# GpSimd's low halves ahead of the gate products, and a reordered even mixer, in a two-block float32 network on one core

## The reference

```python
def even_mixer(x, ...):
    p = x @ w_in
    ...
    o = gla_chunked(q, k, v, log_a)
    o = o * lax.rsqrt(jnp.mean(jnp.square(o), -1, keepdims=True) + LN_EPS) * gla_norm_g
    gla_out = o.reshape(B, T, GLA_VW) * jax.nn.silu(gg)
    ...
    kk = heads(k * rwkv_k_k, RWKV_HEADS)
    kk = kk / jnp.maximum(jnp.sqrt(jnp.sum(jnp.square(kk), -1, keepdims=True)), 1e-12)
    k = k * (1.0 + (a - 1.0) * rwkv_k_a)
    y = rwkv7_scan(r_h, heads(decay, RWKV_HEADS), k_h, v_h, -kk, kk * a_h)
    mu = y.mean(-1, keepdims=True)
    var = jnp.square(y - mu).mean(-1, keepdims=True)
    y = (y - mu) * lax.rsqrt(var + RWKV_LNX_EPS) * rwkv_lnx_g + rwkv_lnx_b
    bonus = jnp.sum(r_h * k_h * rwkv_r_k, -1, keepdims=True) * v_h
    rwkv_out = (y + bonus).reshape(B, T, RWKV_W) * g
    return jnp.concatenate([gla_out, rwkv_out], -1) @ w_out
```

## Time and profile before

| | |
|---|---|
| time, median of 3 runs | 3585.91 us (3582.16 to 3587.43) |
| time of the profiled execution | 3586.25 us |
| its span, instructions | 3584.5 us, 49478 |
| PE busy | 3252.6 us (91%), mean granted clock 0.954 |
| VectorE busy | 2184.6 us (61%) |
| ScalarE busy | 1499.0 us (42%) |
| GpSimd busy | 535.2 us (15%) |
| DMA | 158 GB/s, mean over the span |

### The profile page before, as it was taken

One profiled execution on the slowest core, in us unless ns is written; L12 is line 12 of the kernel. 1 busy time (PEld: TensorE's weight loads), 2 busy tenths in 40 slices (PEclk: granted clock), 3 DMA queues, 4 the chain that ended last, 5 costly groups with the idle time before them and its releaser, 6 DMA issues.

```text
span 3584.5 us, 49478 instructions
## 1 busy us (share of the span) xinstructions
PE 3252.6 (91%) x20412; PEld 2873.0 (80%) x20412; DVE 2184.6 (61%) x3104; ACT 1499.0 (42%) x1677; POOL 535.2 (15%) x275
## 2 busy tenths in 40 slices
...
GB/s 183 138 185 162 212 152 182 151 105 163 181 169 195 157 185 158 132 2 118 165 155 116 113 236 192 187 188 188 153 35 143 176 129 137 153 228 179 188 188 127
DMA packets 87677, 565.23 MB, mean 158 GB/s; under 512 B 10176, under 2 KB 10192, under 8 KB 23584
## 3 DMA queue, kind: packets, MB, share of 16 engines
...
## 4 chain that ended last, share of the span: by engine, by line
PE 46%; DVE 6%; POOL 4%; ACT 4%; issue 1%; DVEq 0%; ACTq 0%
PE bank L1841 7%; PE bank L1843 7%; PE bank L1842 7%; PE bank L1820 6%; PE bank L1821 6%; PE bank L1822 6%; POOL w_lo L1488 3%; ACT w_hi L1935 2%; PE bank L1803 1%; PE bank L1543 1%; PE bank L1544 1%; PE bank L1545 1%; DVE hot_i L2517 1%; PE bank L1567 1%; PE bank L1568 1%
## 5 line engine op out<-in xcount | busy, mean ns | idle before, releaser
L1935 ACT ACTIVATE w_hi<-raw 128x2048 fp32r<-128x2048 f32 x290 | 555.4, 1916 | 838.5 <-PE bank L1843 395.6
L2199 DVE TENSOR_TENSOR w_lo<-raw,w_hi 128x2048 fp32r<-128x2048 f32 x222 | 531.6, 2396 | 609.2 <-ACT w_hi L1935 609.1
L875 DVE TENSOR_TENSOR w_lo<-raw,w_hi 128x2048 fp32r<-128x2048 f32 x202 | 462.4, 2292 | 413.1 <-ACT w_hi L687 409.7
L1820 PE MATMUL bank<-act_hi,w_hi 128*128 128x256 f32 x2048 | 598.8, 292 | 60.8 <-POOL w_lo L1488 55.2
L687 ACT ACTIVATE w_hi<-raw 128x2048 fp32r<-128x2048 f32 x202 | 386.5, 1915 | 545.8 <-PE bank L464 371.4
L1821 PE MATMUL bank<-act_lo,w_hi 128*128 128x256 f32 x2048 | 586.2, 286 | 0.0
L1822 PE MATMUL bank<-act_hi,w_lo 128*128 128x256 f32 x2048 | 585.8, 286 | 0.0
L1820 PEld LDWEIGHTS bank<-act_hi,w_hi 128*128 128x128 f32 x2048 | 399.0, 195 | 66.4 <-POOL w_lo L1488 60.2
L1841 PE MATMUL bank<-w_hi,c_hi 128*128 128x512 f32 x1024 | 405.0, 396 | 0.0
L1842 PE MATMUL bank<-w_lo,c_hi 128*128 128x512 f32 x1024 | 405.0, 395 | 0.0
L1843 PE MATMUL bank<-w_hi,c_lo 128*128 128x512 f32 x1024 | 405.0, 395 | 0.0
...
## 6 DMA issues: line engine op xcount, KB each, us to landing
...
```

What stands on the lines that cost most here:

```text
L875: nc.vector.tensor_tensor(w_lo[:, k % SPLIT, :], raw[:, k % RAW, :], w_hi[:, k % SPLIT, :].bitcast(F32), ALU.subtract).then_inc(lo_ready, 1)
L1820: mm(dst, wh[:, ws], act_hi[:, kk_, :], start=kk_ == 0 and jj == 0, stop=False)
L1935: A.activation(hi_of(k), raw[:, k % RAW, :], ACT.Copy).then_inc(hi_ready, 1)
L2199: V.tensor_tensor(lo_of(k), raw[:, k % RAW, :], hi_of(k).bitcast(F32), ALU.subtract).then_inc(lo_ready, 1)
```

## The change

GpSimd's part. In the gate stage the low half of tile p+1 moves ahead of all weighings of tile p. Two tiles of the even mixer, 12 and 13 (the first output weights), are made by GpSimd instead of VectorE, and GpSimd waits for the step "z" of both halves before the first of them. `lo` moves out of `peer_layer`.

The norms of kk. PE's product with a 128x128 matrix that gave each row's sum over its head in the feature layout becomes one with two columns, which gives 8 sums per token in the token layout. ScalarE's root, VectorE's maximum and reciprocal work on 128x8 instead of 128x512; VectorE spreads the result over 512 columns, and PE transposes it back into PSUM (the new step "norm"), where the product with kk reads it. These instructions stand ahead of the state updates.

The GLA output. PE's `o` waits for the states alone, no more for "tilde" of the first half. ScalarE copies it to `ymix` (step "copied") and takes the squares there. VectorE's scaling is cut into six pieces, one behind the first product of each level.

The end of the chain. `fade[2]` is made behind the chain's first copy. The statistics of the first half stand behind the second new state, its centring behind the third copy, its last two instructions behind the third state.

```diff
+MIX_LO_BY_POOL = (EVEN_OUT, EVEN_OUT + 1)
...
-    _by = any(_t - _first in LO_BY_POOL for _first in PEER_UV)
+    _by = _t in MIX_LO_BY_POOL or any(_t - _first in LO_BY_POOL for _first in PEER_UV)
...
@@ gpsimd
+        pool.wait_ge(rw_pe, TT * RW_PE["z"])
+        for k in MIX_LO_BY_POOL:
+            lo(base + k)
         pool.wait_ge(tr_lo, 8)
         ln_load(0)
...
             for p in range(FIRST_GATED, LAST_GATED + 1):
-                for n, g in enumerate(mid_groups(p) + end_groups(p)):
+                if p + 1 in LO_BY_POOL:
+                    lo(first + p + 1)
+                for g in mid_groups(p) + end_groups(p):
                     if g + HOT < GROUPS:
                         weigh(g + HOT)
-                    if n == 0 and p + 1 in LO_BY_POOL:
-                        lo(p + 1)
@@ tensor
             for f in range(FT):
-                last = mm(psum[4 + t][:, f * P:(f + 1) * P], cst("same_head"), sq[:, f, HALVES[t]], start=True, stop=True)
+                last = mm(psum[4 + t][:, 2 * f:2 * f + 2], sq[:, f, HALVES[t]], cst("half"), start=True, stop=True)
...
+        for t in range(TT):
+            by_dve("norm", t)
+            for f in range(FT):
+                last = nc.tensor.transpose(psum[4 + t][:, f * P:(f + 1) * P], norm[:, t, f * P:(f + 1) * P], ident)
+            last.then_inc(rw_pe, 1)
         pe.wait_ge(even_dve, EVEN_DVE["states"])
-        by_dve("tilde", 0)
...
                 if t and n == 2:
-                    pe.wait_ge(even_dve, EVEN_DVE["gla"])
+                    pe.wait_ge(even_act, EVEN_ACT["copied"])
@@ scalar
             by_pe("bonus", t)
-            do(A.activation(norm[:, t, :], psum[4 + t][:, :], ACT.Sqrt), rw_act)
+            do(A.activation(rnorm[:, t, :], psum[4 + t][:, 0:RH], ACT.Sqrt), rw_act)
         act.wait_ge(even_pe, EVEN_PE["o"])
         for t in range(TT):
+            do(A.activation(ymix[:, t, 0:EW], psum[6 + t][:, :], ACT.Copy), even_act if t else None)
+        for t in range(TT):
             for h in range(GH):
...
@@ vector
         def split_lo(k):
-            if k < total:
+            if k < total and not LO_COUNT[k - base][0]:
...
+        for t in range(TT):
+            by_act("norm", t)
+            if t == 0:
+                by_pe("bonus", TT - 1)
+                do.also(V.tensor_copy(bonus[:, :, :], psum[7][:, 0:TT * RH].rearrange("p (t h) -> p t h", t=TT)))
+            do(V.tensor_scalar(rnorm[:, t, :], rnorm[:, t, :], 1e-12, None, ALU.max))
+            do(V.reciprocal(rnorm[:, t, :], rnorm[:, t, :]))
+            do(V.tensor_copy(norm[:, t, :].rearrange("p (h n) -> p h n", h=RH), bcast(rnorm[:, t, :].unsqueeze(2), [P, RH, RN])), rw_dve)
...
-        def gla_out():
+        def gla_out(n):
+            t, part = n // 3, n % 3
+            if part == 0:
+                dve.wait_ge(even_act, EVEN_ACT["std"])
+                if t == 0:
+                    do(V.reciprocal(small[:, 8:16], small[:, 8:16]))
+            if part == 2:
                 do(V.tensor_tensor(ymix[:, t, 0:EW], ymix[:, t, 0:EW], gsil[:, t, :], ALU.mult), even_dve if t else None)
+                return
+            for h in (2 * part, 2 * part + 1):
...
-            n0 = norm[:, t, :]
-            do(V.tensor_scalar(n0, n0, 1e-12, None, ALU.max))
-            do(V.reciprocal(n0, n0))
-            do(V.tensor_tensor(kk[:, :, ts], kk[:, :, ts], n0.rearrange("p (f s) -> p f s", f=FT), ALU.mult))
+            by_pe("norm", t)
+            do(V.tensor_tensor(kk[:, :, ts], kk[:, :, ts], psum[4 + t][:, :].rearrange("p (f s) -> p f s", f=FT), ALU.mult))
...
-        gla_out()
         eye = cst("eye64")
+        dve.wait_ge(even_pe, EVEN_PE["o"])
...
+            gla_out(n)
...
+            if n == 0:
+                end = (CHUNKS - 1) * CHUNK_T - 1
+                do.also(V.tensor_tensor(fade[2], ...))
+            if n == 2:
+                centre(0)
             if n < CHUNKS - 1:
                 dve.wait_ge(chain_pe, 2 * n + 2)
                 do(V.tensor_tensor(s_all[:, n, :, :], ...), chain_dve)
+            if n == 1:
+                statistics(0)
+            if n == 2:
+                finish(0)
+        statistics(1)
+        centre(1)
+        finish(1)
```

More of the change, by code:

```diff
@@ L225 @@
 LEVEL_STEPS = [f"{s}{n}" for n in range(LEVELS) for s in "xd"]
-RW_PE = steps("bonus", "nat", "lr", "x0", *LEVEL_STEPS[2:], "z", "y")
+RW_PE = steps("bonus", "norm", "nat", "lr", "x0", *LEVEL_STEPS[2:], "z", "y")
 RW_ACT = steps("decays", "norm", "nat", "z", "std")
-RW_DVE = steps("cumsum", "bonus", "tilde", "lr", *LEVEL_STEPS, "stats")
+RW_DVE = steps("cumsum", "bonus", "norm", "tilde", "lr", *LEVEL_STEPS, "stats")
 ODD_PE = steps("it", "index0", "index1", "qt", "logits0", "pt0", "o0", "logits1", "pt1", "o1")
@@ L1252, in second_block @@
     gv = sb("gv", [P, TT, EW], F32, gla)
+    gap2 = sb("gap2", [P, (CHUNKS - 1) * FT * P - TT * EW], F32, gla)
     gsil = sb("gsil", [P, TT, EW], F32, gla)
@@ L1475, in ln_load, with lo @@
             pool.dma_start(ln_rows_at[n][:, 1, :], ln_rows[2 * n + 1].partition_broadcast(P)).then_inc(ln_loaded, 16)
+        def lo(k):
+            pool.wait_ge(hi_ready, k + 1)
+            nc.gpsimd.tensor_tensor(lo_of(k), raw[:, k % RAW, :], hi_of(k).bitcast(F32), ALU.subtract).then_inc(lo_pool, 1)
+        pool.wait_ge(rw_pe, TT * RW_PE["z"])
+        for k in MIX_LO_BY_POOL:
+            lo(base + k)
         pool.wait_ge(tr_lo, 8)
@@ L1483, in peer_layer @@
             first, g0 = base + PEER_UV[layer], GROUPS * layer
-            def lo(q):
-                k = first + q
-                pool.wait_ge(hi_ready, k + 1)
-                nc.gpsimd.tensor_tensor(lo_of(k), raw[:, k % RAW, :], hi_of(k).bitcast(F32), ALU.subtract).then_inc(lo_pool, 1)
             def weigh(g):
@@ L1496, in peer_layer @@
                 if q in LO_BY_POOL:
-                    lo(q)
+                    lo(first + q)
             for g in range(HOT):
@@ L2338, in _ @@
                        even_dve if c == CH * TT - 2 and g == GP - 1 else None)
-        def gla_out():
-            dve.wait_ge(even_act, EVEN_ACT["std"])
-            do(V.reciprocal(small[:, 8:16], small[:, 8:16]))
-            for t in range(TT):
-                for h in range(GH):
-                    hs = slice(h * GDV, (h + 1) * GDV)
-                    do(V.scalar_tensor_tensor(out=ymix[:, t, hs], in0=psum[6 + t][:, hs], scalar=small[:, 8 + t * GH + h:9 + t * GH + h],
-                                              in1=erow[:, EROW["gla_g"]], op0=ALU.mult, op1=ALU.mult))
-                do(V.tensor_tensor(ymix[:, t, 0:EW], ymix[:, t, 0:EW], gsil[:, t, :], ALU.mult), even_dve if t else None)
+        def gla_out(n):
[5 more added lines that the diff above has]
+            if part == 2:
+                do(V.tensor_tensor(ymix[:, t, 0:EW], ymix[:, t, 0:EW], gsil[:, t, :], ALU.mult), even_dve if t else None)
+                return
+            for h in (2 * part, 2 * part + 1):
+                hs = slice(h * GDV, (h + 1) * GDV)
+                do.also(V.scalar_tensor_tensor(out=ymix[:, t, hs], in0=ymix[:, t, hs], scalar=small[:, 8 + t * GH + h:9 + t * GH + h],
+                                               in1=erow[:, EROW["gla_g"]], op0=ALU.mult, op1=ALU.mult))
+            do.settle()
         for t in range(TT):
@@ L2415, in _, with statistics @@
         do.settle()
-        end = (CHUNKS - 1) * CHUNK_T - 1
-        do(V.tensor_tensor(fade[2], bcast(cst("same_head").unsqueeze(1), [P, FT, P]), bcast(pinc[:, :, end:end + 1], [P, FT, P]), ALU.mult))
-        for n in range(CHUNKS):
-            t, c = n // CH, n % CH
-            cs = slice(c * CHUNK_T, (c + 1) * CHUNK_T)
-            dve.wait_ge(chain_pe, 2 * n + 1)
-            do(V.tensor_copy(uu[cs, t, :], psum[4 * t + 1][cs, :]), chain_dve)
-            if n < CHUNKS - 1:
-                dve.wait_ge(chain_pe, 2 * n + 2)
-                do(V.tensor_tensor(s_all[:, n, :, :], psum[4 * t + 2 + c][:, :].rearrange("p (f s) -> p f s", f=FT), fade[n], ALU.mult), chain_dve)
-        for t in range(TT):
+        def statistics(t):
             by_pe("y", t)
```

25 lines of the change are left out of this document (16 added, 9 removed).

## The result

The changed kernel takes 3535.82 us (median of 4 runs, 3533.29 to 3541.45) against 3586.55 us of the kernel before on the same chip: ratio 0.9863, 95% interval 0.9846 to 0.988. Its profiled execution took 3533.58 us against 3586.25, 52.7 us less. The first row of its page, busy time and share of the span, says that PE works no less, but stands less and runs faster: 92% of a span of 3531.9 us, with a mean granted clock of 0.959.

The account below looks back on a forecast made before the run. PE, by far the busiest engine, was taken as the bound, losing time to waits and clock drops. Gate stage 30.2, clock 16.1 and mixer 6.6 sum to 52.9 us, from 3586.25 to 3533.4; range 3517 to 3553.

Parts of the forecast that it names:

- Gate stage: Expert stage: GpSimd's low half ahead of the weighings shortens ten PE stalls a layer, 30.2 us over two layers.
- The foreseen exception: Gate stage: VectorE's low half gets ahead of the first weighing, perhaps in a layer's last pair; 1.4 us a pair.
- The clock: Gate stage: all 11 drops of PE's granted clock behind the stalls go, 16.1 us; other bound 0.
- The mixer: Even mixer, along VectorE's path: 13.1 - 1.2 - 8.3 - 2 + 5.0 = 6.6 us gained, bounds 16 and 2.
- (c): Mixer: GLA output waits only for the states, which end at 1520.2 instead of 1522.6; output ends at 1527.5.
- (d): Mixer: ScalarE's copies, squares and root take 7.3 us; triangular products start at 1535.4 instead of 1548.45, gain 13.1 us.
- (e): Mixer: scaling the GLA output in six pieces between the levels costs VectorE's path 1.2 us.
- (f): Mixer: GpSimd's two low halves hold VectorE's bonus terms, delaying the chain's first copy; loss 8.3 us, bounds 0 and 9.1.
- the rival of the unheld VectorE: Mixer: VectorE isn't held at the bonus terms, so the mixer gives 16 us and the time is 3524; chance 0.13.
- The foreseen sign: Mixer: single instructions of the bonus terms last 4 to 5 us.
- (g): Mixer: after standing about 8 us PE restarts the chain at the lower clock level, costing 2 us (0 to 3).
- (h): Mixer: the first half's statistics move into idle gaps of the chain, so the second half's start earlier; gain 5.0 us.

Follow-up runs that it names:

- Experiment 1: The kernel before with only the gate-stage edit, GpSimd's low half ahead of the weighings of its tile: 3538.87 us, ratio 0.9868.
- experiment 5: The changed kernel with GpSimd's gate-stage low half behind the second weighing of a pair: 3648.12 us, ratio 1.0178.
- experiment 2: The changed kernel with the gate-stage edit undone, so the mixer's edits alone: 3581.24 us, ratio 0.9985.
- Experiment 3: The changed kernel with the mixer's two low halves made by VectorE again, ahead of the v shift: 3527.03 us, ratio 0.9835.
- experiment 4: The changed kernel with GpSimd's two mixer low halves started behind ScalarE's root instead of behind the z products: 3527.82 us, ratio 0.9832.
- experiment 9: The changed kernel with one of GpSimd's two mixer low halves given back to VectorE: 3534.76 us, ratio 0.9858.
- experiment 7: The changed kernel with statistics, centring and scaling of the first half put back behind the chunk chain: 3540.42 us, ratio 0.9879.
- experiment 6: The changed kernel with VectorE also making the low halves of the odd tiles 27 to 47 of the expert stage: 3513.4 us, ratio 0.9804.

## Why the prediction was right

3533.4 us was forecast and 3535.8 measured. The mechanism of each large term was right, but that the sum came so close is partly luck: by the profiles the terms give 28 + 16.1 + 3.5, some 48 us for the forecast's 52.9, and the profiled execution reaches 52.7 only with the 4.2 us from code that the change doesn't touch. The terms, in the prediction's order:

- **Gate stage, 30.2 us.** The ten waits fell by 15.2 us in the first layer, and by as much in the second. The foreseen exception came, once a layer, in the last pair, where the stall is 1.29 us: 1.0 us each (1.4 foreseen), costed at nothing. Net some 28 us.
- **The clock, 16.1 us.** 46.5 us gained in the two stretches, less 30.4 for the ten stalls in each, leave 16.1. Experiment 1 confirms the sum of both terms (47.3 against 46.3), experiment 5 the cause: the number and length of the drops rise with the stall. Why 9 of the 20 stalls of before had none stays open.
- **The mixer, 6.6 us,** was the weak term: 3.5 in the profiles, 4.9 by experiment 2. Its stated bounds, 16 and 2, don't follow from its own steps either, which give 16.9 and 4.8; the measured 3.5 lies below these. Its steps, with times counted from each kernel's second `kt`:
  - (c) The states were to be done 2.4 us earlier than before. They were only 0.2 us earlier, as VectorE waited 0.42 + 1.99 us for PE. The low halves at the earlier trace rows had covered this: without them the products must be ready early, and PE was just then at the lower level, as the windows of 6.69 us behind that `kt` show, first after, then before:

```profile
1505.12:1511.81 6.69, 5.94 (x27) 5.58 (x29) 5.54 (x13) 1.93 (x4) 0.00 (x0) 0.50 0.01 2
```

```profile
1509.31:1516.00 6.69, 5.75 (x32) 4.67 (x32) 6.62 (x5) 2.75 (x4) 0.00 (x0) 0.74 0.36 130
```

  - (d) The GLA output took 6.4 us, not 7.3, so the triangular products start 12.0 us earlier, not 13.1; and VectorE gets their result 11.1 us earlier, as they took 3.6 us from 1532.28.
  - (e) The pieces in the levels cost 0.75 (1.2).
  - (f) The hold was the step with the widest bounds, and its 8.3 us were measured as 7.8: the first copy of the chain comes at 1594.47. The bonus terms are held like the product of the earlier trace rows, so the rival of the unheld VectorE falls. The foreseen sign is there too: two single bonus terms take 4.54 and 4.53 us, one behind each low half. By the Trainium skill's "SBUF — State Buffer", "Who interferes with whom", a VectorE instruction with two SBUF inputs had to be held so, and the trace agrees. VectorE's turn between the two low halves is worth little here: it is a whole product of 2.29 us in the earlier trace rows and only one of the short terms in this place, so GpSimd's second starts at once (9.48 us for both, against 2 x 4.55) and holds the next term. Experiments 3, 4 and 9 settle it: 10.17 us with two low halves, 5.90 with one, 1.65 with none.
  - (g) The restart at the lower level was mis-sized, 2 us (0 to 3) where the chain became 4.0 longer (16.75 to 20.71). By experiment 7 the statistics in it are 0.1 of that, so 3.9 are the clock. Experiment 3 bears this out. There PE doesn't stand, its clock is at the full level, and from the first copy's product on the chain takes 16.1 us with the statistics, against 16.0 in the kernel before. (Its 17.87 us from copy to copy hold another 1.0 us in which PE is still busy with earlier products.) The windows of the chain, first after, then before, then of experiment 3, end in PEclk, DMA share and GB/s:

```profile
1594.47:1615.18 20.71, 19.97 (x160) 15.96 (x161) 10.31 (x34) 0.30 (x1) 0.00 (x0) 0.78 0.08 32
```

```profile
1601.16:1617.91 16.75, 16.75 (x187) 13.69 (x182) 4.14 (x6) 0.00 (x0) 0.00 (x0) 1.00 0.01 2
```

```profile
1588.69:1606.56 17.87, 17.87 (x199) 14.72 (x199) 10.30 (x34) 0.30 (x1) 0.00 (x0) 1.00 0.01 2
```

  - (h) The statistics gave 4.9 between last copy and end (5.0) and cost the chain 0.1. The whole mixer differs by 3.5 us in the profile of experiment 7, as the changed kernel has another 0.6 us of PE's lower level in the chain and is 0.7 us slower ahead of it, where the edit of experiment 7 changes nothing; in its time it is 4.6 to 5.7.

  Together: 11.1 - 0.75 - 7.8 - 4.0 + 4.9 = 3.5.

Two of the misses in the mixer, (c) and (g), are PE's clock: it was considered, but sized at half, where the change makes a stall, and not considered where the change takes away the work that had covered PE's slower products.

## What to carry over

Work that is taken off a waiting engine and given to GpSimd isn't gone: look what VectorE reads from SBUF while GpSimd's long instruction runs, and start that one while VectorE waits or works on PSUM. In a merged row of short instructions, ask for the single ones: an average of 1.27 us hid two of 4.5. Here the same two instructions cost 8 us at one place and nothing at another. A stall of the busiest engine costs its length and, here behind 11 of 20 stalls of 2.1 to 2.9 us and behind every one of 4.2 and more, the clock as well; so it pays first to shorten stalls that recur, even if none goes away entirely. And before an engine's helper is relieved of work, compare both engines' lengths of the one operation: 4.5 us late hurts more than 2.3 us of a busy engine, as experiment 6 shows.

## What the runs showed of the chip

- GpSimd and VectorE took turns on SBUF instruction by instruction, whatever their lengths. Each low half of GpSimd (4.5 us) held one VectorE instruction that reads two SBUF tiles: two of the eight bonus terms took 4.54 and 4.53 us, the others 0.27, so that the eight took 10.17 us in place of 1.66. In the earlier trace rows it is a product of 2.29 us that gets in between.
- The reverse exists too: VectorE's low half, 0.05 us ahead of the weighing, kept its 2.29 us, while the weighing took 3.14 in place of 1.04.
- With stalls of 4.2 us and more PE's clock was at 1.2 GHz for some 6.8 us in 17 of 20 pairs, some 1.3 of them still in the stall; with 2.1 to 2.9 us it was for 3.4 us or not at all.
- Narrow outputs saved PE next to nothing: at the full clock eight products with 2 columns took 1.03 us in the changed kernel (L1650, first half), eight with 128 columns 1.14 before.
